# Half-job signals, scan products inside jobs, and a convolution LayerNorm with a provisional shift

## The reference

```python
def hybrid_mixer(u, ...):              # first block
    z, xbc, dt_raw, v = split(u @ w_in)
    xbc = silu(causal_depthwise_conv(xbc))            # 4 taps, 12 tiles of 128 channels
    y = ssd_chunked(xs, dt, a, bm, cm)                # scan over 4 chunks of 128 tokens
    y = rmsnorm((y + d_skip * xs) * silu(z)); ... @ w_out

def conformer_conv(u, conv_w, conv_b, g, b):          # second block, first layer ("a")
    a, gl = split(u);  h = a * sigmoid(gl)            # 1536 channels = 12 tiles
    h = depthwise_conv(h, conv_w) + conv_b            # 31 taps
    return silu(layer_norm(h, g, b))                  # mean and variance over the 1536 channels

# each layer of the second block: memory attention beside it, then
x = layer_norm(ALPHA * x + (y * silu(gate)) @ w_out, pg, pb)
```

## Time and profile before

| | us |
|---|---|
| median of 3 runs | 1732.8 (1732.42 to 1736.16) |
| profiled execution, its time | 1733.19 |
| its span in the trace | 1730.6 |
| TensorE busy | 1678.9 (97%) |
| GpSimd busy | 1049.2 (61%) |
| VectorE busy | 912.4 (53%) |
| ScalarE busy | 555.8 (32%) |

### The profile page before, as it was taken

The page is one execution under the profiler, slowest core; times in us unless marked ns, Lnnn a source line. Parts: engine busy times, 40 slices in busy tenths (PEclk is TensorE's granted clock), DMA queues, the critical chain, the costliest instruction groups (busy, mean ns, idle before and its releaser), DMA issues.

```text
span 1730.6 us, 22639 instructions
## 1 busy us (share of the span) xinstructions
PE 1678.9 (97%) x8087; PEld 1369.2 (79%) x8087; DVE 912.4 (53%) x1413; ACT 555.8 (32%) x972; POOL 1049.2 (61%) x775
## 2 busy tenths in 40 slices
PE   7999999999999999999999999999999999999997
PEld 5887897788978888888877878876878778777785
DVE  5322947673445222222258998987356784443415
ACT  4421246420322100100123445746122244553203
POOL 7567663466647766766795877771467553333562
PEclk9999999999999999999999999999999999999999
DMA  6333333223233333333244322221433221121221
GB/s 203 105 115 98 123 98 113 83 88 103 88 137 97 97 98 97 97 97 98 79 123 109 99 77 98 73 83 40 143 90 98 90 74 56 49 69 55 73 86 49
DMA packets 191272, 162.08 MB, mean 94 GB/s; under 512 B 9684, under 2 KB 187472, under 8 KB 190672
## 3 DMA queue, kind: packets, MB, share of 16 engines
q1 hardware_dynamic: 190984, 160.84, 29.8%
q10 hardware_dynamic: 200, 0.06, 0.0%
HBM read 155.60 MB, written 4.23 MB: 92 GB/s over the span
## 4 chain that ended last, share of the span: by engine, by line
PE 81%; DVE 9%; issue 5%; ACT 2%; POOL 2%; DVEq 1%; DMA 0%; SPq 0%; ACTq 0%; POOLq 0%
PE g_bank L864 57%; PE g_bank L879 7%; PE g_bank L889 4%; DVE t_bank L2511 2%; PE t_bank L1392 1%; PE t_bank L1382 1%; POOL w_lo L748 1%; DVE acc L2191 1%; PE g_bank L1277 1%; PE t_bank L1112 1%; PE t_bank L1152 1%; PE t_bank L1184 1%; PE t_bank L1215 1%; PE t_bank L1236 1%; DVE acc L2227 1%
## 5 line engine op out<-in xcount | busy, mean ns | idle before, releaser
L748 POOL TENSOR_TENSOR w_lo<-w_raw,w_hi 128x512 fp32r<-128x512 f32 x416 | 571.6, 1405 | 8.7
L735 POOL TENSOR_SCALAR w_hi<-w_raw 128x2048 fp32r<-128x2048 f32 x104 | 203.1, 1952 | 528.1 <-issue 224.5
L864 PE MATMUL g_bank<-x_hi,w_hi 128*128 128x512 f32 x1248 | 495.2, 397 | 5.1 <-DVEq L2105 3.8
L864 PE MATMUL g_bank<-x_hi,w_lo 128*128 128x512 f32 x1248 | 486.0, 389 | 0.0
L864 PE MATMUL g_bank<-x_lo,w_hi 128*128 128x512 f32 x1248 | 485.8, 389 | 0.0
L864 PEld LDWEIGHTS g_bank<-x_hi,w_hi 128*128 128x128 f32 x1248 | 234.4, 188 | 59.2 <-issue 9.1
L864 PEld LDWEIGHTS g_bank<-x_lo,w_hi 128*128 128x128 f32 x1248 | 234.5, 188 | 49.2 <-issue 2.2
L864 PEld LDWEIGHTS g_bank<-x_hi,w_lo 128*128 128x128 f32 x1248 | 234.3, 188 | 49.1
L2511 DVE SCALAR_TENSOR_TENSOR t_bank<-hc,cols,t_bank 128x512 f32<-128x512 f32 x280 | 186.5, 751 | 2.3 <-DVE hc L2489 2.3
L791 POOL TENSOR_TENSOR w_lo<-w_raw,w_hi 128x512 fp32r<-128x512 f32 x80 | 101.0, 1297 | 68.7 <-ACT w_hi L1784 68.7
L864 PE MATMUL g_bank<-y_hi,w_hi 128*128 128x512 f32 x332 | 130.4, 393 | 1.4 <-ACTq L1648 1.4
(11 more groups left out here) (442 smaller groups left out, 2888.8 us busy)
## 6 DMA issues: line engine op xcount, KB each, us to landing
w_raw<-w_gate_up SPq DMA_DIRECT2D x44, 512.0 KB, 5.0
w_raw<-a_w_in SPq DMA_DIRECT2D x44, 512.0 KB, 4.4
w_raw<-b_w_in SPq DMA_DIRECT2D x38, 512.0 KB, 4.3
w_raw<-w_in SPq DMA_DIRECT2D x28, 512.0 KB, 4.8
w_raw<-w_kv SPq DMA_DIRECT2D x16, 512.0 KB, 4.4
w_raw<-w_out_mix SPq DMA_DIRECT2D x16, 512.0 KB, 6.2
w_raw<-w_down SPq DMA_DIRECT2D x16, 512.0 KB, 4.0
w_raw<-a_w_out SPq DMA_DIRECT2D x16, 512.0 KB, 4.4
```

Source lines behind the costliest of these rows:

```text
L735: nc.gpsimd.tensor_scalar(w_hi[:, par], w_raw[:, par], 1.0, 0.0, ALU.mult, ALU.add).then_inc(pool_chain, 1)
L748: last = nc.gpsimd.tensor_tensor(w_lo[:, par, s], w_raw[:, par, s], w_hi[:, par, s].bitcast(F32), ALU.subtract)
L864: last = nc.tensor.matmul(g_bank[:, 2 * pair + f, 0:n], ww[:, k0 + k, ws], xk, start=(k == 0 and q == 0), stop=(k == kt - 1 and q == 2))
```

## The change

- **Half signals.** `products_T` can signal `w_half` when its first half is done. VectorE then convolves the first tile of `xbc_1` to `xbc_5` at that signal, and in both output LayerNorms it adds tile 6 to the residual, centres it and adds it to the sums at the half of the last job; tile 7 follows at the job's end. The sums leave the last job; four products in all stand behind it, in place of two inside and four behind.
- **Scan.** `state`, `yoff` and `ydiag` move from ahead of job `wo_pool + c` into it, behind its steps 1, 2 and 3.
- **Convolution's LayerNorm.** A provisional mean m0 of tiles 0 and 2 is made by two products behind the seventh `a_glu` job. Tiles 5, 7, 9, 10 and 11 get -m0 as the addend of their tap 1 on VectorE, the others by additions of GpSimd. ScalarE squares the shifted tiles during the jobs; GpSimd adds up six shifted tiles into `c_sum` and seven squares into `q_sum`, one or two additions a job, behind its taps (now 4 a job up to job 11, then 3). Ten products (for both sums together) stand at steps 6 and 12 of the last gate job. The variance is made as mean of squares less square of mean; the rest of the mean is subtracted from tiles 0 and 1 by VectorE and from 2 to 11 by GpSimd, in two parts, ahead of and behind the split of output job 1's weights.
- `mem_max` and the reciprocal move four taps later in tiles 7, 9 and 10. `out_weights_hi/lo` move to k = 5, 6, 10 and 11.
- Two pairs of counters are merged into one; that changes no order.

```diff
-        more = min((4 if j % 2 == 0 else 3) if j >= 4 else 0, len(CONV_POOL) * TAPS - n)
+        more = min((4 if j < 12 else 3) if j >= 4 else 0, len(CONV_POOL) * TAPS - n)
...
+            def shift(k, nth):
+
+                pool.wait_ge(mean_ready, 1)
...
+                nc.gpsimd.tensor_tensor(conv_tile(k), conv_tile(k), less_m0[:], ALU.add).then_inc(shifted, 1)
+                pool.wait_ge(shifted, nth)
...
+            def norm_share(j):
+
+                if j == 11:
+                    shift(0, 1)
+                    shift(2, 2)
+                elif j == 12:
+                    shift(4, 3)
+                    shift(6, 4)
+                elif j == 13:
+                    sum_tile(6, 5, first=4)
+                    sum_square(0, 2, 6)
...
             for j in range(a0 + 2, a1):
                 rest(j, j % 2)
                 for n in TAPS_AFTER[j - a0]:
                     tap(n)
+                norm_share(j - a0)
+            shift(3, 19)
+
+            def less_d(k0, k1):
+
+                pool.wait_ge(mean_ready, 2)
+                for k in range(k0, k1):
+                    nc.gpsimd.tensor_tensor(conv_tile(k), conv_tile(k), mean[:], ALU.subtract).then_inc(shifted, 1)
+
             pool.nop().then_inc(pool_chain, a1 - a0 - 2)
-            for i in range(2):
-                job(a1 + i, i, 32 * (a1 // 2) + 32, a1 + i - 1)
+            job(a1, 0, 32 * (a1 // 2) + 32, a1 - 1)
+            less_d(2, 8)
+            job(a1 + 1, 1, 32 * (a1 // 2) + 32, a1)
+            less_d(8, CT_)
...
+                        if half is not None and f == 0 and k == kt - 1:
+                            last.then_inc(half, 1)
...
+            def scan(c):
+
+                def turn(step):
+                    if step == 1 and c < CHUNKS - 1:
+                        pe.wait_ge(xdt_ready, c + 1)
...
+                    elif step == 2 and c:
+                        pe.wait_ge(prev_ready, c)
...
+                    elif step == 3:
+                        pe.wait_ge(xdt_ready, c + 1)
+                        pe.wait_ge(m_ready, c + 1)
...
-                jobs(JOBS["wo_pool"] + c, 1, lambda par: products_T(par, y_hi, y_lo))
+                jobs(JOBS["wo_pool"] + c, 1, lambda par: products_T(par, y_hi, y_lo, between=scan(c)))
...
+            jobs(JOBS["a_glu"] + 1, 6, lambda par: products_T(par, x_hi, x_lo))
+            b = bank(TASKS["a_m0"])
+            pe.wait_ge(conv_done, 2)
+            nc.tensor.matmul(b, ones[:], hc[:, 0, HP:HP + T], start=True, stop=False)
+            nc.tensor.matmul(b, ones[:], hc[:, 2, HP:HP + T], start=False, stop=True).then_inc(t_ready, 1)
...
+            jobs(JOBS["a_gate"] + 7, 1, lambda par: products_T(par, x_hi, x_lo, between=conv_sums))
...
+                    both = [bank(ln + 1), bank(ln + 2)]
+                    for q, b in enumerate(both):
+                        pe.wait_ge(ln_sums, 2 * layer + 1 + q)
+                        nc.tensor.matmul(b, ones[:], ln_s[:, q, :], start=True, stop=False)
+                    pe.wait_ge(ln_cent, DT * layer + 8)
+                    nc.tensor.matmul(both[0], ones[:], hT[:, 7, :], start=False, stop=True).then_inc(t_ready, 1)
+                    pe.wait_ge(ln_sq, DT * layer + 8)
+                    nc.tensor.matmul(both[1], ones[:], nring[:, 1, :], start=False, stop=True).then_inc(t_ready, 1)
...
                 weights_hi(j + 2)
+                if n == 1:
+                    square_of(4, q_ring[1], 3)
...
+                elif n == 3:
+                    square_of(8, q_ring[1], 8)
...
-                dve.wait_ge(w_used, j + 1)
+                if f == 0 and t:
+                    dve.wait_ge(w_half, t // 2)
+                else:
+                    dve.wait_ge(w_used, j + 1)
...
-                taps(tile, 0, 11)
+                taps(tile, 0, 15)
                 mem_max(0, i)
-                taps(tile, 11, 17)
+                taps(tile, 15, 21)
                 mem_reciprocal(0, i)
-                taps(tile, 17, TAPS)
+                taps(tile, 21, TAPS)
...
+            dve.wait_ge(mean_ready, 2)
+            link(v.tensor_tensor(cacc[:], mean[:], mean[:], ALU.mult))
+            done(v.scalar_tensor_tensor(rstd[:], ready(TASKS["a_var"]), 1.0 / CW, cacc[:], ALU.mult, ALU.subtract),
+                 cvar_ready, t_free[BANK[TASKS["a_var"]]])
+            for k in range(2):
+                c = hc[:, k, HP:HP + T]
+                ins = v.tensor_tensor(c, c, mean[:], ALU.subtract)
+            link(ins)
             dve.wait_ge(root_ready, 1)
             link(v.reciprocal(rstd[:], rstd[:]))
             for k in range(CT_ + 2):
                 if k < CT_:
+                    if k >= 2:
+                        dve.wait_ge(shifted, 19 + k - 1)
...
-                if k == 9:
+                if k == 6:
                     out_weights_lo(2)
                     add_out(JOBS["a_out"], 0, 1)
-            out_weights_lo(3)
+                if k == 11:
+                    out_weights_lo(3)
+                    add_out(JOBS["a_out"], 1, 2)
```

More of the change, by code:

```diff
@@ L359, in program @@
         ya0_hi = at("ya0_hi", [P, 4, T], rS, F32R)
-        sqa = [nring[:, 0, :], nring[:, 1, :]] + [at(f"sqa{i}", [P, T], rY + 26112 + 8 * KB + i * 2 * KB)[:] for i in range(4)]
+        less_m0 = mean
+        c_sum = rstd
+        q_sum = at("q_sum", [P, T], rY + 26112 + 14 * KB)
+        q_ring = [at(f"q_ring{i}", [P, T], rY + 26112 + 18 * KB + i * 2 * KB) for i in range(2)]
+        q_3 = at("q_3", [P, T], rY + 26112 + 12 * KB)
         pacc = [at(f"pacc{i}", [P, T], rY + 26112 + i * 2 * KB) for i in range(2)]
@@ L1035, in _ @@
                     if i == 1:
-                        products_T(j % 2, x_hi, x_lo, w=wts, between=turns).then_inc(w_used, 1)
+                        products_T(j % 2, x_hi, x_lo, w=wts, between=turns, half=w_half).then_inc(w_used, 1)
                     else:
-                        products_T(j % 2, x_hi, x_lo, w=wts).then_inc(w_used, 1)
+                        products_T(j % 2, x_hi, x_lo, w=wts, half=w_half).then_inc(w_used, 1)
                     for q in range(2):
@@ new lines, in scan @@
+            def scan(c):
+                def turn(step):
+                    if step == 1 and c < CHUNKS - 1:
+                        pe.wait_ge(xdt_ready, c + 1)
+                        for g in range(GROUPS):
+                            b = bank(TASKS[f"state{c}"] + g)
+                            nc.tensor.matmul(b, b_nat[:, c, g * STATE:(g + 1) * STATE], xdd[:, g * HPG:(g + 1) * HPG, :],
+                                             start=True, stop=True).then_inc(t_ready, 1)
+                    elif step == 2 and c:
+                        pe.wait_ge(prev_ready, c)
+                        for g in range(GROUPS):
+                            b = bank(TASKS[f"yoff{c}"] + g)
+                            nc.tensor.matmul(b, cT[:, g, c * P:(c + 1) * P], state_into(c, g, g + 1),
+                                             start=True, stop=True).then_inc(t_ready, 1)
+                    elif step == 3:
+                        pe.wait_ge(xdt_ready, c + 1)
+                        pe.wait_ge(m_ready, c + 1)
+                        for g in range(GROUPS):
+                            b = bank(TASKS[f"ydiag{c}"] + g)
+                            for i in range(HPG):
+                                h = g * HPG + i
+                                last = nc.tensor.matmul(b[:, i * HD:(i + 1) * HD], decay_of(c, h), xdt[:, h, :], start=True, stop=True)
+                            last.then_inc(t_ready, 1)
+                return turn
@@ L1811, in _, with square_of @@
                 tap_products(a0 + i + 2)
+                if i == 6:
+                    b = ready(TASKS["a_m0"])
+                    link(copy(less_m0[:], b, -1.0 / (2 * P)))
+                    act.nop().then_inc(t_free[BANK[TASKS["a_m0"]]], 1)
+                    act.nop().then_inc(mean_ready, 1)
+            def square_of(k, into, pool_done):
+                if k in CONV_DVE:
+                    act.wait_ge(conv_done, CONV_DVE.index(k) + 1)
+                if pool_done:
+                    act.wait_ge(shifted, pool_done)
+                nc.scalar.activation(into[:], hc[:, k, HP:HP + T], ACT.Square).then_inc(csq_ready, 1)
             def qm_evac(layer, i, base):
@@ L2507, in taps @@
                         ins = v.tensor_scalar(a(k), h(k), wk, w(COL["a_conv_b"]), ALU.mult, ALU.add)
+                    elif k == 1 and isinstance(tile, int):
+                        ins = v.scalar_tensor_tensor(a(k), h(k), wk, less_m0[:], ALU.mult, ALU.add)
                     elif k == 1:
@@ L2631, in add_up @@
                         for q, new, first in ((0, hT[:, k, :], hT[:, 0, :]), (1, nring[:, k % 2, :], nring[:, 0, :])):
-                            ins = v.tensor_tensor(ln_s[:, q, :] if k == 5 else sums[q], first if k == 1 else sums[q], new, ALU.add)
-                            if k == 5:
```

(2 more changed lines are left out.)

189 lines of the change are left out of this document (107 added, 82 removed).

## The result

The changed kernel takes 1740.45 us (median of 20 runs, 1736.93 to 1744.95); the kernel before, on the same chips, 1734.98 (20 runs). The ratio is 1.0028, 95% interval 1.0017 to 1.0038: some 5 us slower, where 1729.5 was forecast. The profiled execution takes 1740.64 us with a span of 1738.9, 8.3 more than the span before.

A forecast was written before the change was run, and what follows sets the result against it. The prediction took TensorE, busy 1678.9 of 1730.6 us, as the bound. Its terms, -12.0 + 3.1 + 0 + 9 + 1 - 3.3 - 1.2, summed to -3.4 us, giving 1729.5 us, range 1719 to 1738.

The forecast's parts named there:

- Products of mean and variance: Convolution's LayerNorm: 24 products go, ten come back inside the last gate job, so TensorE saves 12.0 us.
- Maximum: Memory attention: maximum four taps later and a square in ScalarE's order lengthen TensorE's wait, +3.1 us, bounds +2 and +4.
- m0 and GpSimd's load: Convolution: two products for m0 taken as 0 (bound 1.7 us); GpSimd's additions fit its jobs, 0 (1 to 3 if late).
- Behind the statistics: Behind the convolution's LayerNorm sums: VectorE and GpSimd operations collide over SBUF and delay output job 1, +9 us.
- turns taken all the way: Rival: each VectorE operation meeting GpSimd lets one pass; 13 us behind the statistics, 5 in the scan, 1737.5 us, chance 0.20.
- 0, 8 and 13: Collision cost in us behind the statistics: unhindered 0, VectorE keeping its turn some 8, turns all the way some 13.
- Scan: Scan stage: VectorE sets the pace and its chain starts 2.7 us later, mostly regained; +1 us, within 0 to +5.
- sign for being right: Scan: waits there as long as before, one of the signs listed as showing the forecast right.
- the 1.27 us: Scan: VectorE's wait for the job, which the forecast placed in the last chunk only, 1.27 us.
- Half signals: Half-job signals: nothing in the front; gains in the output LayerNorms, -3.3 us in layer b and -1.2 us in layer a.
- LayerNorm b: Layer b's output LayerNorm: job ends 1.7 us earlier and the mean stands 2.7 us behind it, not 4.3; -3.3 us.
- LayerNorm a: Layer a's output LayerNorm: the same 1.7 us but no wait to fill; -1.2 us, bounds -0.5 and -1.7.

The follow-up runs named there:

- e14: Kernel before with only the memory maximum and reciprocal of tiles 1 to 3 moved to taps 15 and 21: 1738.54 us, ratio 1.0025.
- e10: Changed kernel with the memory maximum and reciprocal back at taps 11 and 17: 1736.78 us, ratio 1.0010 to the kernel before.
- e1: Kernel before with only the scan's products moved inside their wo_pool job, at steps 1, 2 and 3: 1743.28 us, ratio 1.0055.
- e13: Changed kernel with ydiag at step 2 of the job, right behind yoff: 1734.13 us, ratio 0.9992 to the kernel before.
- e8: Kernel before with only the scan's products moved inside their job, ydiag at step 2 right behind yoff: 1734.30 us, ratio 1.0005.

## Why the prediction was wrong, step by step

- **Products of mean and variance, -12.0:** right. The last gate job ends where -12.0 puts it (1179.51 + 10.31 of the earlier trace rows, 13.6 that came in ahead of it, less 12.0, make 1191.4; it ends at 1191.28).
- **Maximum, +3.1:** right, 3.3 by the wait (3.85 against 0.54), 2.6 of it the four taps (e14) and 0.7 the square (the 1.2 us of e10).
- **m0 and GpSimd's load, 0:** right. No wait of a gate job for GpSimd's rests is in the trace, and the profile's offset doesn't grow over `a_glu`.
- **Behind the statistics, +9:** the mechanism was right and the size near: the wait grew by 10.4. The recorded rival of turns taken all the way describes it better, each operation losing about 1.0 us, for as long as GpSimd has work. The 9 were a choice between 0, 8 and 13, so that they come near the 10.4 is in part luck. The Trainium skill, SBUF — State Buffer, section "Who interferes with whom", says that the two exclude each other for a whole instruction; the trace agrees nearly: with a stream on both sides neither keeps the other out, and 1.67 us from start to start hold one VectorE operation (0.60) and most of one of GpSimd's (1.25), a little less than the 1.85 of both.
- **Scan, +1:** too low. It is 2.7 to 3.0 of work and waits. The forecast counted how late `ydiag` comes in chunk 0 and took the later chunks as covered by VectorE's own order; at full clock VectorE idles 0.6 us in front of it in the changed kernel's first cycle and in the second of e1, since the step and `ydiag` itself stand between `yoff` and its next read, and the collision takes 1.7 once. Its sign for being right, waits in the scan as long as before, did not come: 5.2 us in place of 2.6. It also misread: the 1.27 us are the wait of the last chunk but one, the last has 5.24 at 340.17.
- **Half signals:** front 0, right; LayerNorm b -3.3, measured -3.7; LayerNorm a -1.2, measured -1.8. In the changed kernel the mean is ready for ScalarE at 1722.46, 2.8 us behind the job's end (2.7 forecast), where the earlier trace rows has 4.3.
- **The step that failed: the sum has no term for TensorE's clock.** It counts a wait as its length and puts the clock behind it at nothing, without a reason. The runs showed 8.4 us of it in the profiled pair. In the profiled pair the terms without clock come to -0.3, 3.1 above the -3.4 forecast (scan 1.7, statistics 1.4, front 0.8, maximum 0.2, less 1.0 at the LayerNorms); the clock adds 5.1 in the scan, 1.7 behind the maximum, 1.6 at the output job, 8.4 in all. The medians are 5.5 apart, less than the profiled pair's 7.45, since some executions of the kernel before lose clock as well (in 11 of 30 its mean granted clock was 0.992 to 0.994 and the time 1738.6 to 1741.9, in the rest 0.995 to 0.998 and 1732.4 to 1735.4). By the ratio the change costs 4.9 us, 8.3 above the forecast: with 3.1 from the other terms, some 5 are left for the clock. The row for it was there: before, the window from 1191 shows 0.96, behind the wait of 2.9 us at the first output job. The Trainium skill, TensorE: Matmul & The Clock Gate, section "HAM oscillation — how this bites in real kernels", warns of idle gaps between matmuls for this reason; the trace agrees for the waits of 3.2 to 3.9 us at the maximum, and behind the shorter ones of the scan the clock fell in some profiles and not in others.

The forecast's rival "turns all the way" (1737.5) named the place and the 13 us, and put 5 us in the scan. It is the nearest of the cases, still 3 us low, and it too had nothing for the clock. That the lower clock follows from the wait is shown for the maximum (seven of seven against none of nine, and it came and went with the edit in e14 and e10). For the scan it is shown that it went with the step (e13), but not by which wait; why some executions lose it there with short waits, and others keep it behind the wait of 2.8, stays open.

## What to carry to other kernels

Before work is moved to GpSimd, see which stretch it will run in: under a stream of two-input VectorE operations it costs VectorE as much as if VectorE did the work itself and more, ten moved subtractions added 8 us to the critical chain, and giving them back to VectorE, 6 us of work, shortened it. In a chain that alternates between two engines, place the products in the order and at the distance in which the other engine reads them; a single job step between two of them cost 2.4 us of work, and with the clock that went with it 9 us in the medians (e1 against e8). And price a new wait of TensorE with the slower clock that may stand behind it: 1.7 us behind every wait of 3.2 to 3.9 us at the maximum here, behind those of 2.1 to 2.9 in some profiles and not in others. What it costs depends on who sets the pace behind the wait: only 0.2 us (7.33 against 7.1) where the products wait for VectorE's tiles anyway.

## What was not expected of the hardware

VectorE and GpSimd advanced one for one over 15 us: 1.5 to 1.7 us from start to start on VectorE, seven times in a row, with GpSimd at 1.60 to 1.65 us an operation, against 0.60 and 1.25 alone. Neither kept its turn for good, as VectorE does beside the 3.58 us rounding of the earlier trace rows. And TensorE's clock fell behind waits of 2.1 to 3.9 us in the midst of stages where it is otherwise busy without a break, in three profiles even behind one of 0.79; behind a wait of 13.1 us the job lost no more to it (7.49 us for 24 products) than behind one of 2.9 (7.33).
